# The row phase's convolution as one product over 32 tokens and 31 taps, then a sum over the taps

## What is computed

```
[q|k|v|c] = RMSNorm(x) W_in                      # 1024 x (3*512 + 2*512)
o_attn = stick_breaking_attention(q, k, v)       # 8 heads of 64, causal
h = a * sigmoid(gate)                            # a, gate: halves of c, 512 wide each
h = depthwise causal convolution of h, 31 taps, + conv_b
o_conv = silu(layer_norm(h))
h = x + [RMSNorm(o_attn) | o_conv] W_out
xn = RMSNorm(h)
experts, gates = product-key search of xn Wq     # 8 heads x 16 experts a token
y = h + sum_k gates_k * gelu(xn . u_tab[e_k]) * v_tab[e_k]
```

## Time and profile before

| | us |
|---|---|
| median of 3 runs | 2847.38 (2847.22 to 2849.18) |
| the profiled execution, its own time | 2849.06 |
| span of the profiled execution | 2847.2 |
| DVE busy | 2154.0 (76%) |
| PE busy | 2232.5 (78%) |
| POOL busy | 1978.4 (69%) |
| start of the row part of chunks 1 and 7 on DVE (the copy of L2250) | 521.19 and 2493.66 |

### The profile page before, as it was taken

One profiled execution on the slowest core, in us unless ns is written; L12 is line 12 of the kernel. 1 busy time (PEld: TensorE's weight loads), 2 busy tenths in 40 slices (PEclk: granted clock), 3 DMA queues, 4 the chain that ended last, 5 costly groups with the idle time before them and its releaser, 6 DMA issues.

```text
span 2847.2 us, 30140 instructions
## 1 busy us (share of the span) xinstructions
PE 2232.5 (78%) x7669; PEld 760.9 (27%) x7669; DVE 2154.0 (76%) x5486; ACT 822.4 (29%) x1998; POOL 1978.4 (69%) x2086
## 2 busy tenths in 40 slices
PE   8999978778667776788768886787868787666667
PEld 4644433223212231232312331132312322111111
DVE  5889979568887788778887788788888858755452
ACT  3223422331124221352115421263115611111111
POOL 1446656777777777777777777777777777777775
PEclk9999989989868896789868897699868997666667
DMA  7269999999999999999999999999999999999998
GB/s 252 86 268 412 392 391 361 419 418 419 419 419 417 416 419 418 406 406 419 419 417 409 395 419 419 416 403 418 419 419 402 415 419 419 414 419 420 415 418 353
DMA packets 322020, 1124.75 MB, mean 395 GB/s; under 512 B 36097, under 2 KB 43289, under 8 KB 321848
## 3 DMA queue, kind: packets, MB, share of 16 engines
q0 software_dynamic: 294912, 1073.87, 93.1%
q1 hardware_dynamic: 26920, 48.94, 4.8%
q10 hardware_dynamic: 16, 0.00, 0.0%
HBM read 1114.30 MB, written 8.39 MB: 394 GB/s over the span
## 4 chain that ended last, share of the span: by engine, by line
DMA 38%; issue 20%; POOL 13%; PE 11%; DVE 6%; ACT 2%; POOLq 0%; ACTq 0%; DVEq 0%
DMA w_kept<-in_peer_u,experts 15%; DMA ring_v<-in_peer_v,v_experts 10%; DMA ring_v<-in_peer_v,gate_rows 8%; POOL w_kept L1818 7%; PE psum L1923 6%; POOL ring_v L1818 6%; DMA w_kept<-in_peer_v,gate_rows 2%; DVE w_kept L2261 2%; DMA w_kept<-in_peer_v,v_experts 1%; PE psum L560 1%; PE psum L1849 1%; DVE log_keep L2184 1%; PE psum L1304 1%; DVE acc L2217 1%; DMA qT_spill<-qT_out 1%
## 5 line engine op out<-in xcount | busy, mean ns | idle before, releaser
L1923 PE MATMUL psum<-ring_v,diag 128*64 128x512 f32 x3224 | 1134.6, 788 | 482.6 <-DMA ring_v<-in_peer_v,v_experts 226.4
L2261 DVE CUSTOM_DVE_ANT_0 w_kept<-w_kept,psum 128x1024 f32<-128x1024 f32 x896 | 1087.9, 1218 | 491.8 <-DMA w_kept<-in_peer_u,experts 486.7
L1818 POOL DMA_INDIRECT w_kept<-in_peer_u,experts x896 | 847.7, 946 | 282.2 <-issue 226.6
L2084 ACT ACTIVATE diag<-stacked,weights 128x64 f32<-128x64 f32 x992 | 303.0, 339 | 790.7 <-PE psum L1923 577.6
L1923 PEld LDWEIGHTS psum<-ring_v,diag 128*64 128x64 f32 x3224 | 211.4, 161 | 1175.4 <-issue 672.9
L1818 POOL DMA_INDIRECT ring_v<-in_peer_v,v_experts x430 | 406.5, 945 | 147.7 <-issue 112.1
L1818 POOL DMA_INDIRECT ring_v<-in_peer_v,gate_rows x376 | 357.4, 950 | 157.3 <-issue 96.9
L1923 PE MATMUL psum<-w_kept,diag 128*64 128x512 f32 x744 | 242.0, 736 | 92.3 <-DMA w_kept<-in_peer_v,gate_rows 40.1
L560 PE MATMUL psum<-w_sb,xnT 128*128 128x512 f32 x640 | 285.7, 602 | 0.3 <-ACT xnT L809 0.3
L2217 DVE SCALAR_TENSOR_TENSOR acc<-conv_in,taps,acc 128x128 f32<-128x128 f32 x720 | 204.8, 346 | 0.5
L504 POOL DMA_INDIRECT w_kept<-in_peer_u,experts x128 | 120.3, 940 | 83.9 <-issue 30.8
(11 more groups left out here) (279 smaller groups left out, 2009.2 us busy)
## 6 DMA issues: line engine op xcount, KB each, us to landing
w_kept<-in_peer_u,experts POOLq DMA_INDIRECT x1024, 13.0
w_sb<-in_w_in SPq DMA_DIRECT2D x4, 2048.0 KB, 17.0
ring_v<-in_peer_v,v_experts POOLq DMA_INDIRECT x430, 13.1
ring_v<-in_peer_v,gate_rows POOLq DMA_INDIRECT x376, 13.0
x_in<-in_x SPq DMA_DIRECT2D x8, 512.0 KB, 9.2
w_kept<-in_w_out SPq DMA_DIRECT2D x1, 4096.0 KB, 14.8
h_res<-in_x SPq DMA_DIRECT2D x8, 512.0 KB, 6.5
w_kept<-in_peer_wq SPq DMA_DIRECT2D x2, 2048.0 KB, 8.6
```

The costliest lines, as they stand in the source:

```text
L1818: nc.gpsimd.indirect_dma_start(slot(kind, n), None, peer_u[0] if kind == "u" else peer_v[0], bass.IndirectOffsetOnAxis(index[:, e:e + 1], ...
L1923: last = nc.tensor.matmul(y_ps[d * GROUP:(d + 1) * GROUP, j * BANK:(j + 1) * BANK], diag[:, e % DIAGS, :], slot("v", n)[:, d * BANK:(d + 1 ...
L2084: nc.scalar.activation(diag[:, e % DIAGS, :], S.stacked[:, :], ACT.Copy, scale=weights[:, e:e + 1]).then_inc(diagonal, step_of(c, e))
L2261: nc.vector.tensor_tensor_reduce(out=row, in0=row, in1=hn, scale=1.0, scalar=0.0, op0=ALU.mult, op1=ALU.add, accum_out=dots[:, e:e + 1]).t ...
```

## The change

`convolve(f, n)` now has 33 pieces instead of 31 taps. For each of the 4 channel blocks and each of the 4 groups of 32 tokens there are two DVE instructions: a product of 32 tokens x 31 taps = 992 elements into `relu_z[0]` (L2221 after; `conv_in` is read with overlapping windows, `taps` repeated for each token), and a `reduce_sum` over the 31 taps into 32 elements of `acc` (L2224 after). The 33rd piece adds the bias to all of `acc` (512 elements, L2209 after). Each piece waits for the one before it. All 33 are run for chunk f + 1 in front slots 48 to 80 of chunk f, one a slot; none is left in the attention. Phase 0 is not changed.

```diff
-OWN_TAPS = 8
+TAP_T = 32
+TAP_PIECES = 2 * CB * P // TAP_T
+TAP0 = ATT_END + 5
...
-        def convolve(f, t):
-
-            if t == 0:
+        def convolve(f, n):
+
+            start, block = TAP_OPS * f, [[1, TAP_T], [1, TAPS]]
+            product = S.relu_z[0][:, 0:TAP_T * TAPS].rearrange("p (t k) -> p t k", k=TAPS)
+            if n == TAP_PIECES:
+                dve.wait_ge(S.tapped, start + n)
+                nc.vector.tensor_tensor(acc[:, :, :], acc[:, :, :], spread(b_conv, [[1, CB], [0, P]]),
+                                        ALU.add).then_inc(S.tapped, TAP_OPS - TAP_PIECES)
+                return
+            c, at = n // 2 // (P // TAP_T), n // 2 % (P // TAP_T) * TAP_T
+            if n == 0:
                 dve.wait_ge(S.c_in, 16 * (f - 1))
-                if later(f):
-                    dve.wait_ge(S.conv_T, f)
+                dve.wait_ge(S.conv_T, f)
+                if f == 2:
+                    dve.wait_ge(S.projected_v, CHUNKS)
             else:
-                dve.wait_ge(S.tapped, TAP_OPS * f + t * CB)
-            for c in range(CB):
...
+                dve.wait_ge(S.tapped, start + n)
+            if n % 2 == 0:
+                nc.vector.tensor_tensor(product, spread(conv_in[:, c, at:at + 1], block),
+                                        spread(taps[:, c, 0:1], [[0, TAP_T], [1, TAPS]]), ALU.mult).then_inc(S.tapped, 1)
+            else:
+                nc.vector.reduce_sum(acc[:, c, at:at + TAP_T], product, AXX).then_inc(S.tapped, 1)
...
-            if f > 1:
-                for t in range(TAPS - OWN_TAPS, TAPS):
-                    if s == TAP_SLOTS[t]:
-                        convolve(f, t)
-            if f < CHUNKS - 1:
-                for t in EARLY_TAPS:
-                    if s == TAP_SLOTS[t]:
-                        convolve(f + 1, t)
+            if f < CHUNKS - 1 and TAP0 <= s <= TAP0 + TAP_PIECES:
+                convolve(f + 1, s - TAP0)
```

More of the change, by code:

```diff
@@ L81 @@
 FRONT_SLOTS = GATES + 1
-EARLY_TAPS = range(TAPS - OWN_TAPS)
-TAP_SLOTS = ([ATT_END + 5 + n * (SEARCH[0] - ATT_END - 5) // len(EARLY_TAPS) for n in EARLY_TAPS]
-             + [ATT0 + ATT_SUM + 2 + ATT_STEP * n for n in range(OWN_TAPS)])
 FIRST_SLOT = ATT_END - LEAD
@@ L90 @@
 KEY_HALVES = 2 * PH
-assert len(TAP_SLOTS) == TAPS and TAP_SLOTS[-1] < CONV_T and FRONT_SLOTS <= SLOTS
+assert TAP0 + TAP_PIECES < SEARCH[0] and FRONT_SLOTS <= SLOTS
 def spread(view, dims):
@@ L365, in phase0 @@
     qT_stored, hT_stored, h_kept = sem("qT_stored"), sem("hT_stored"), sem("h_kept")
-    S.kT_copied, S.qT_stored, S.hT_stored = kT_copied, qT_stored, hT_stored
+    S.kT_copied, S.qT_stored, S.hT_stored, S.projected_v = kT_copied, qT_stored, hT_stored, projected[V]
     w_second = sem("w_second")
@@ L2202, in norm_o @@
             nc.vector.tensor_scalar(o_norm, o_ps, S.stat[:, 3:4], None, ALU.mult).then_inc(S.o_normed, 1)
-        def convolve(f, t):
-            if t == 0:
+        def convolve(f, n):
[8 more added lines that the diff above has]
+            if n == 0:
                 dve.wait_ge(S.c_in, 16 * (f - 1))
-                if later(f):
-                    dve.wait_ge(S.conv_T, f)
-            else:
-                dve.wait_ge(S.tapped, TAP_OPS * f + t * CB)
-            for c in range(CB):
[L2213 to L2219, removed]
+                dve.wait_ge(S.conv_T, f)
+                if f == 2:
+                    dve.wait_ge(S.projected_v, CHUNKS)
+            else:
+                dve.wait_ge(S.tapped, start + n)
[4 more added lines that the diff above has]
+                nc.vector.reduce_sum(acc[:, c, at:at + TAP_T], product, AXX).then_inc(S.tapped, 1)
         def ln_stats(f):
```

## The result

| | before | after |
|---|---|---|
| median, us | 2848.55 (2844.20 to 2852.28, 20 runs) | 2852.24 (2850.03 to 2856.45, 20 runs) |
| profiled execution, its own time | 2849.06 | 2851.43 |
| span of the profiled execution | 2847.2 | 2849.6 |
| start of the row part of chunks 1 and 7 | 521.19 and 2493.66 | 525.31 and 2496.88 |

The ratio is 1.0014, with a 95% interval of 1.0008 to 1.0020: slower by 3.7 us, which is clear of the noise but within the 0.2% that the prediction counts as no change. The forecast was 2851.7. Between the two traces the span grows by 2.4 us: 4.1 up to the row part of chunk 1, -0.9 in the row phase, and -0.8 from the row part of chunk 7 on (353.5 and 352.7 us).

A forecast was written before the change was run, and what follows sets the result against it. Gathers at 419 GB/s were taken to bound the row parts, and DVE's list the stretch from 394 to 460 us. Terms 5.8 + 1.5 - 3 = +4.3 us on the median 2847.38 gave 2851.7, range 2842 to 2861.

The forecast's parts named there:

- The start: Chunk 0's row part: a longer DVE list delays the side rows, `add_side` and all later gathers, +5.8 us.
- rival 3: Start costs nothing because PE's work, not the side rows, sets v row 64: -1.5 us, 2845.9; chance 10%.
- The piece price: On DVE, each product or sum of 992 elements costs 1.10 us from start to start.
- the side row of 393.79: Chunk 0's row part: waits ahead of this row hold the additional work, so it doesn't move.
- their delay costs nothing: Chunk 1's experts come at 497 us, POOL asks at 520.62: over 20 us of cover, so no cost.
- Slots 48 to 80: Chunks 2 to 6: 11.6 us more DVE work fits in 15.7 us of waits; small lags cost +1.5 us.
- Wrong: GB/s below 415 in those slots: Sign against the prediction: DMA rate below 415 GB/s in the 33 piece slots, where 418 or more was expected.
- Attention: Chunks 2 to 6: DVE is 1.05 us lighter a head, which heals a fifth of the dips, -3 us.
- 16 us of dips: Row parts of chunks 2 to 6: twelve windows below 410 GB/s were estimated to lack 16 us in all.
- DVE's part is some quarter: Attention dips: PE is late by itself too, so DVE's share in them is some quarter.
- Rival 1: The late DVE is behind most attention dips, so all 16 us come back: -8.7 us, 2838.7; chance 13%.
- Rival 2: DVE becomes the bound in slots 48 to 80, with pieces at 1.23 us: 2865; chance 17%.

The follow-up runs named there:

- experiment 7: Changed kernel, but chunk 2 convolved by the four-instruction taps of before in their old slots: ratios to the kernel before 0.9985 and 0.9987 (2845.11 us).
- experiment 6: Kernel before with all 31 taps early (front slots 48 to 79), chunk 2's in slots 94 to 124 of chunk 1: ratios 1.0062 and 1.0000 (2848.96 us).
- experiment 1: Changed kernel, but products of chunks 3 to 7 read their second factor from PSUM: ratios to the kernel before 0.9985, 0.9975 and 1.0006 (2851.07 us).
- experiment 3: Changed kernel, but in chunks 3 to 7 a second product with two SBUF inputs replaces each sum: ratios to before 1.0050 and 1.0112 (2880.90 us).

## Why the prediction was right, and by what

**The start: right, perhaps somewhat too large.** +5.8 was forecast. `add_side` moved by 5.2, the row part of chunk 1 by 4.1; the three traces with the new list against the two with the old one give 5.3 and 4.7 on average. The chain was the right one, and undoing chunk 2 alone brought the time back (experiment 7), which also answers rival 3. The piece price held; what was off is the side row of 393.79, which came 0.9 us earlier instead of standing still. What the forecast didn't see is that this bound is one-sided: the landing of the v rows stands 1 to 3 us behind it (experiment 6). The step "their delay costs nothing", with 20 us of cover for the experts, held for the change, where they came 6 us later than in the earlier trace rows:

```profile
502.86 0.38 DVE L1566 SCALAR_TENSOR_TENSOR experts<-actT 128x128 int32<-128x128 bf16 x1
```

The same cover is what experiment 6 ran out of, with a delay of 25 us.

**Slots 48 to 80: the term failed, and by another mechanism.** +1.5 was forecast, from DVE lagging and POOL waiting for it. DVE had 4.8 us of waits where about 4 were forecast, and POOL none over 0.6 us in this stretch, so the lag that the term priced left no trace. But products held POOL's gathers, of which the working had nothing: sixteenths 8 to 10 of the row parts of chunks 1 to 5 lost, by (419 - GB/s) / 419 x 20.6 summed over those below 410, 15 us. "Wrong: GB/s below 415 in those slots" was the sign given, and it came: 405.

**Attention: the term was too small.** -3 was forecast, a fifth of the 16 us of dips. The prediction's 16 us of dips is 16.4 by the same sum. Outside the piece slots the changed kernel has only 4 us of dips left, so some 12 healed. "DVE's part is some quarter" isn't confirmed: with VectorE's attention just as light (15.03 against 15.08 us busy), but POOL fast again, the dip was back at 361 GB/s (experiment 1), and at 367 in experiment 6. So no run shows that DVE's lighter list heals any of it. The row of POOL says what the dip is: 15 gathers in the window, not 17. As I read it, it healed because POOL, behind by then, asked for its buffers later, when PE had freed them; that was not tested by itself. Over all six row parts the dips come to 16.4 us before, 19.0 after, 14.8 with the PSUM factor and 46.4 with the second product: the change moved them from the attention to the piece slots and took none away.

**The sum of these two was right by luck.** Both errors have one cause. POOL had some 40 us of waits in the row phase, the products took 39, and the waits disappeared. The row phase came out at -0.9 us; +1.5 - 3 = -1.5 was forecast. Nothing in the prediction says that the two amounts would be alike; with 26 us more in the gathers the row phase grew by 27, far off the forecast. Rival 1 (2838.7) took the healing for a gain; it healed, and nothing was gained. Rival 2 had the bound on the wrong engine: the one that had come near it is POOL, as experiment 3 shows with +27 us.

**Open.** Why 40 us of waits on POOL and none give the same row phase is only argued. Before, the queue of gathers is long (14.0 us to landing in the late piece slots), after, it is short (6.3 us), and the rate beside the dips is mostly 418 to 420 in both. The issues of gathers from 2020 to 2040 us, with KB and the median us to landing, of before and after:

```profile
w_kept<-in_peer_u,experts POOLq DMA_INDIRECT x9, 14.0
```

```profile
w_kept<-in_peer_u,experts POOLq DMA_INDIRECT x8, 6.3
```

This fits two limits that lie almost on each other, POOL's 1.24 us a gather and the transfers. But a wait of 2.13 us at 1850 us in experiment 1 stands beside a dip though the gathers had 12.9 us to landing, and the one of 3.03 us in the earlier trace rows left 419 GB/s. The changed kernel has no wait at that place, and no dip at 7.8 us to landing. What decides when a wait is paid wasn't found.

## What to carry to other kernels

Before a VectorE instruction with two large SBUF inputs is put beside indirect gathers, count the gathers that will start inside it: each waits for its end. One input in PSUM or a sum avoids it, and with short pieces little of it is left. And when such a cost appears, measure the slack of the engine that pays (its idle time less its issue time, over the whole phase): here 40 us were free and the 26 behind them were not. A list that bounds a stretch should be probed both ways, since the next bound may stand 1 to 3 us behind it. And a total that comes out as forecast says little of its terms: two of three were wrong here.

## What the runs showed of the hardware

- A gather lasts 0.94 us beside a sum, a dot with one factor in PSUM, or a product with one factor in PSUM, and up to 1.95 us when it starts just behind the start of a 1.19 us product of two SBUF inputs. It then ends 0.80 to 0.82 us behind the product's end (67 gathers at 80 products). Taps of 128 columns, which also read two SBUF inputs, leave the mean of the u gathers at 0.95; single ones last up to 1.10 in the 33 slots of before.
- A product of 992 elements with overlapping windows and repeated taps costs what a plain one does: 1.19 us, 1.10 from start to start.
- The kernel before took 2848 us in the runs of the result and on the third and fourth chip, and 3272 and 3240 on the first two, where the mean rate was 342 to 348 GB/s and an edit's sign could be another (0.9964 against 1.0014 for the changed kernel).
